# A fused two-block transformer kernel: the second block's first norm taken by halves of the tokens, with its context rows normed ahead

## The reference

```python
# first block, layer 1, its end
x = x + rmsnorm(y, g_post_mix[1]);  h_ = rmsnorm(x, g_pre_ffn[1])
y = conv_ffn(h_, ...)                        # up (2 x 2816 columns), conv, silu*val, down
x = x + rmsnorm(y, g_post_ffn[1])
# second block, layer 0, its start: h = x (512 tokens), hc = ctx (256 tokens)
mx = split(silu(c) @ w_mod[0] + b_mod[0], 6);  mc = split(silu(c_ctx) @ w_mod[0] + b_mod[0], 6)
ax = rmsnorm_2(h,  norm1_g[0]) * (1 + mx[1]) + mx[0]
ac = rmsnorm_2(hc, norm1_g[0]) * (1 + mc[1]) + mc[0]
mixing_layer(ax @ w_in[0], ac @ w_in[0], ...)
```

## Time and profile before

| | before |
|---|---|
| runs | 2862.49, 2864.14, 2866.07 us (median 2864.14) |
| profiled execution | 2862.76 us, its span 2861.0 us |
| TensorE busy | 2795.2 us, 98% |
| VectorE, ScalarE, GpSimd busy | 62%, 40%, 6% |
| HBM traffic | 94 GB/s over the span |

### The profile page before, as it was taken

How to read it: one execution, slowest core, us unless ns; L and a number is a source line. 1 busy time by engine, 2 the same in 40 slices (tenths; PEclk the granted TensorE clock), 3 DMA queues, 4 the chain that set the end, 5 groups by cost and what they waited for, 6 DMA issues and landing times. The chain is left out here.

```text
span 2861.0 us, 35838 instructions
## 1 busy us (share of the span) xinstructions
PE 2795.2 (98%) x14584; PEld 2371.3 (83%) x14584; DVE 1772.3 (62%) x2696; ACT 1141.6 (40%) x1734; POOL 157.8 (6%) x172
## 2 busy tenths in 40 slices
PE   9999999999899999999989999999999999999998
PEld 8658888888477888889956899999998975788887
DVE  6678866678768667676676565335534137674563
ACT  5255524443545334342265333223323236553342
POOL 0101000010210000100020100000000002100001
PEclk9999999999999999999999999999999999999999
DMA  5303242343122342425610121121121121232322
GB/s 208 112 16 125 90 146 97 95 135 124 38 81 90 105 137 94 140 100 206 219 49 30 59 74 64 57 72 59 62 61 64 66 100 52 75 106 84 113 85 85
DMA packets 85205, 269.96 MB, mean 94 GB/s; under 512 B 9264, under 2 KB 14256, under 8 KB 84656
## 3 DMA queue, kind: packets, MB, share of 16 engines
q1 hardware_dynamic: 85040, 267.66, 28.1%
HBM read 265.52 MB, written 2.10 MB: 94 GB/s over the span
## 5 line engine op out<-in xcount | busy, mean ns | idle before, releaser
L1213 PE MATMUL PS<-HH,WH 128*128 128x512 f32 (+2 forms) x3124 | 1027.5, 362 | 16.2 <-DVE HL L849 6.1
L1213 PE MATMUL PS<-HL,WH 128*128 128x512 f32 (+2 forms) x3124 | 1017.3, 359 | 0.0
L1213 PE MATMUL PS<-HH,WL 128*128 128x512 f32 (+2 forms) x3124 | 1017.2, 359 | 0.0
L1009 DVE TENSOR_TENSOR WL<-STAGE,WH 128x1024 fp32r<-128x1024 f32 (+2 forms) x420 | 482.9, 1152 | 465.0 <-ACT WH L1003 464.6
L1003 ACT ACTIVATE WH<-STAGE 128x1024 fp32r<-128x1024 f32 (+2 forms) x420 | 407.9, 974 | 619.2 <-DMA STAGE<-in_w_down 272.7
L1213 PEld LDWEIGHTS PS<-HH,WH 128*128 128x128 f32 x3124 | 577.7, 188 | 91.5 <-DVE HL L849 8.7
L1213 PEld LDWEIGHTS PS<-HL,WH 128*128 128x128 f32 x3124 | 578.6, 188 | 64.5 <-issue 2.4
L1213 PEld LDWEIGHTS PS<-HH,WL 128*128 128x128 f32 x3124 | 578.3, 188 | 63.0
L1213 PE MATMUL PS<-GH,WH 128*128 128x512 f32 (+2 forms) x902 | 301.7, 364 | 0.0
L1213 PE MATMUL PS<-GL,WH 128*128 128x512 f32 (+2 forms) x902 | 300.4, 362 | 0.0
L1213 PE MATMUL PS<-GH,WL 128*128 128x512 f32 (+2 forms) x902 | 300.4, 362 | 0.0
(11 more groups left out here) (233 smaller groups left out, 2434.2 us busy)
## 6 DMA issues: line engine op xcount, KB each, us to landing
STAGE<-in_w_up SPq DMA_DIRECT2D x176, 512.0 KB, 3.2
MODBUF<-in_w_mod SPq DMA_DIRECT2D x96, 512.0 KB, 4.1
STAGE<-in_w_in SPq DMA_DIRECT2D x84, 512.0 KB, 3.3
STAGE<-in_w_down SPq DMA_DIRECT2D x64, 384.0 KB, 3.1
STAGE<-in_w_down SPq DMA_DIRECT2D x64, 320.0 KB, 2.9
STAGE<-in_w_out SPq DMA_DIRECT2D x32, 512.0 KB, 4.4
BM<-in_na_bias SPq DMA_DIRECT2D x24, 256.0 KB, 2.5
CR<-in_const_ret SPq DMA_DIRECT2D x2, 1152.0 KB, 5.2
```

What stands on the lines that cost most here:

```text
L1009: dve.tensor_tensor(WL[unit.slot][:, 0:size], STAGE[unit.slot][:, 0:size], WH[unit.slot][:, 0:size].bitcast(F32), ALU.subtract).then_inc(w ...
L1213: ins = pe.matmul(self.acc(tile, col, tn, p), w[:, c:c + P], r[:, k, t0:t0 + tn], start=(k == 0 and m == 0 and not (joined and p)), stop=( ...
```

## The change

What it does, in five parts:

1. `CrossHead` takes the place of `NormHead` for `norm_in2(0)`, and the last down projection of layer 1 is halved too (`halved=half`). A new `CtxPrep` runs inside that projection: ScalarE squares the context chunks, two in each of tiles 0 to 3; GpSimd adds them, two behind its own add of each of the tiles 1 to 4; TensorE takes their mean at the start of tile 5, waiting for the last of these adds (`csq_added`); and at tiles 4, 5 and 6 the context chunks are normed (T, HH, HL, 256 columns). After the last down tile `CrossHead.begin` first multiplies the context columns for the first three `in2(0)` tiles, with the sums of the squares of X's first half among them, then does half 0 of the tokens with the sums of half 1 between its chunks, then half 1. The idle matmuls of this crossing are gone.
2. `mods`: two products for tiles 1 to 4 of `out1` in place of one for tiles 0 to 5, and two for all 8 tiles of the first down projection of each layer in place of 6. The products of the last down projection of layer 1 are thereby gone from it.
3. The copy to COND and the load of the context move from that last down projection to `out1(1)`; products from then on read COND.
4. Where the token count changes, the accumulators keep their turns, and a tile waits only for the tiles that used its banks.
5. `pe_chunk` takes a part of the columns and whether it is the last; the first three tiles of `in2(0)` have their columns in one piece (`flat`).

```diff
+        class CrossHead(Head):
+
+
+            begins = True
+
+            def __init__(self, scale, shift, hi, lo, gain):
+                super().__init__(hi, lo, SEQ)
+                self.scale, self.shift, self.gain = scale, shift, gain
+
+            def plan(self, run):
+                self.h0, self.t0, self.y0, self.x0, self.before = run.n_h, run.n_t, run.n_y, run.n_x, run.squares
+                self.halved, self.steps, self.joined = True, [], False
+                run.n_h, run.n_t, run.n_y, run.n_x = run.n_h + 24, run.n_t + 24, run.n_y + 16, run.n_x + 16
+                self.ctx_norm = Rstd(run, CTX, [(0, SEQ, CTX)])
+                self.first = Rstd(run, SEQ, self.before.parts)
+                self.norm = Rstd(run, SEQ, self.before.parts)
+
+            def step(self, i):
+
+                return i % DC, slice(SEQ, TOK) if i < DC else self.rows(i // DC - 1), 1 if i < DC else 0
+
...
+            def act(self, act):
+                last = self.before.seg.tiles[-1]
+
+                def squared(i):
+                    p, c = divmod(i, DC)
...
+                        for u in self.early:
+                            self.run.split_high(act, u)
+                        self.before.wait_mean(act, 1)
+                        self.first.act(act, 1)
+                for c in range(2):
+                    squared(DC + c)
+                act.wait_ge(xsq_summed.sem, xsq_summed.at(self.x0 + DC))
+                self.norm.act(act)
+                for c in range(DC):
+                    self.high(act, DC + c)
+                    if c + 2 < DC:
+                        squared(DC + c + 2)
+                act.wait_ge(xsq_summed.sem, xsq_summed.at(self.x0 + 2 * DC))
+                self.norm.act(act, 1)
+                for c in range(DC):
+                    self.high(act, 2 * DC + c)
+
+            def dve(self, dve):
+                last = self.before.seg.tiles[-1]
+
+                def scaled(i):
```

`CrossHead.act` ends as it begins, with `self.high` for half 1. `CrossHead.dve` has the same order in scales, adds, T and HL. Its TensorE part and `CtxPrep`:

```diff
+                              start=(c == 0), stop=(c == DC - 1)).then_inc(xsq_summed.sem, 1)
+
+                ctx(0, first[0:2])
+                ctx(1, first[0:2])
+                self.before.mean(pe, 1)
+                for k in range(2, DC):
+                    if k < 6:
+                        squares_summed(2 * k - 4)
+                        squares_summed(2 * k - 3)
+                    ctx(k, first[0:2])
+                for k in range(DC):
+                    ctx(k, first[2:])
+                for p in range(2):
                     for c in range(DC):
-                        pe.wait_ge(xsq_done.sem, xsq_done.at(self.x0 + c + 1))
-                        for t0, tn in ranges(self.tokens):
-                            ins = pe.matmul(PS[2][:, t0:t0 + tn], MEAN[:], SQ[c % 2][:, t0:t0 + tn],
-                                            start=(c == 0), stop=(c == DC - 1))
-                        ins.then_inc(xsq_summed.sem, 1)
-                    idle(pe, 24, 3)
+                        self.wait_lo(pe, DC + DC * p + c)
+                        for tile in first:
+                            self.run.pe_chunk(pe, tile, c, 0, halves_of(SEQ)[p], final=p == 1)
+                        if p == 0:
+                            squares_summed(DC + c)
...
+            def pool(self, pool, t):
+                if t <= 4:
+                    for c in (2 * t - 2, 2 * t - 1):
+                        if c == 0:
+                            continue
+                        pool.wait_ge(csq_done.sem, csq_done.at(c + 1))
+                        if c > 1:
+                            pool.wait_ge(csq_added.sem, csq_added.at(c - 1))
+                        first = SQ[0] if c == 1 else SQSUM
+                        pool.tensor_tensor(SQSUM[:, SEQ:TOK], first[:, SEQ:TOK], SQ[c % 2][:, SEQ:TOK],
+                                           ALU.add).then_inc(csq_added.sem, 1)
+
+            def pe(self, pe, run, tile):
+                if tile.t == 5:
+                    pe.wait_ge(csq_added.sem, csq_added.at(DC - 1))
+                    pe.matmul(PS[2][:, 0:CTX], MEAN[:], SQSUM[:, SEQ:TOK], start=True, stop=True).then_inc(csq_summed.sem, 1)
 
```

The banks, the products and the copy:

```diff
                         if tiles and tiles[-1].seg.tokens != seg.tokens:
-                            turns, changed, users = 0, len(tiles), {}
+                            behind = 1 + next(i for i, acc in enumerate(columns(TOK)) if tiles[-1].banks[-1] in acc[2])
+                            turns = behind * len(accs) // 3
...
-                            tile.after = max([changed] + [users.get(bank, 0) for bank in banks])
...
+                            tile.after = max(users.get(bank, 0) for bank in tile.banks)
...
+                if keeps:
+                    self.from_x = next(product.n for tile in tiles for product in tile.products if product.kept)
+                    self.mod_loads[tiles[2].units[0].u + ring] = [None]
...
+                            if self.keeps and tile.n == 1:
                                 act.activation(COND[:], X[:, :, SEQ:TOK], ACT.Copy).then_inc(cond_kept.sem, 1)
...
-                            mods=lambda t: 1 if t < 6 else 0, halved=1)]
...
+                            mods=lambda t: 2 if 1 <= t < 5 else 0, halved=1)]
...
-                            ready=half * HALF, mods=lambda t: 2 if t < 6 else 0, out_dve=add_y if half else to_y, squares=y_rows if half else None,
-                            halved=1 if half and l == 0 else 0)]
+                            ready=half * HALF, mods=lambda t, half=half: 2 if half == 0 or t < 6 else 0,
+                            out_dve=add_y if half else to_y, squares=y_rows if half else None,
+                            prep=prep if half else None, halved=half)]
```

More of the change, by code:

```diff
@@ L245, in columns @@
             if tokens == SEQ:
[L246 to L247 removed]
+                return [(PS[i], h * SEQ, [2 * i + h]) for i in (0, 1, 3) for h in range(2)]
+            return [(PS[i], 0, [2 * i, 2 * i + 1]) for i in (0, 1, 3)]
         def tap(seg, t, k):
@@ L800, in act @@
             def act(self, act):
-                n = self.tokens
                 self.before.wait_mean(act)
-                if self.gain:
-                    self.first.act(act)
-                    act.wait_ge(ctx_in.sem, ctx_in.at(16))
-                    for c in range(DC):
-                        act.wait_ge(added.sem, added.at(self.y0 + c + 1))
-                        if c > 1:
-                            act.wait_ge(xsq_summed.sem, xsq_summed.at(self.x0 + c - 1))
-                        act.activation(SQ[c % 2][:, 0:n], X[:, c, 0:n], ACT.Square).then_inc(xsq_done.sem, 1)
-                    act.wait_ge(xsq_summed.sem, xsq_summed.at(self.x0 + DC))
                 self.norm.act(act)
@@ L821, in dve @@
             def dve(self, dve):
-                if self.gain:
-                    self.first.wait(dve)
-                    scale_y(dve, self.gain, 0)
-                    for c in range(DC):
-                        if c + 1 < DC:
-                            scale_y(dve, self.gain, c + 1)
-                        dve.wait_ge(y_scaled.sem, y_scaled.at(self.y0 + c + 1))
-                        dve.tensor_tensor(X[:, c, 0:SEQ], X[:, c, 0:SEQ], Y[:, c, :], ALU.add).then_inc(added.sem, 1)
                 def normed(i):
@@ L914, in __init__ @@
                 self.n_h = self.n_t = self.n_y = self.n_x = self.n_hid = self.n_late = 0
-                self.squares, self.units, tiles, turns, changed, users = None, [], [], 0, 0, {}
+                self.squares, self.units, tiles, turns, users = None, [], [], 0, {}
                 for head, segments in parts:
@@ L949, in __init__ @@
                                 if waiting and waiting[0].l == (seg.weights is a["w_in2"]):
+                                    waiting[0].kept = keeps and tile.n > 1
                                     tile.products.append(waiting.pop(0))
@@ L1198, in dve_out, with pe_chunk @@
                     seg.out_dve(dve, t, tile.ps[:, tile.col:]).then_inc(acc_free.sem, 1)
-            def pe_chunk(self, pe, tile, k, p=None):
+            def pe_chunk(self, pe, tile, k, p=None, part=None, final=True):
                 seg = tile.seg
-                parts = [halves_of(seg.tokens)[p]] if p is not None else parts_of(seg.tokens)
-                joined = tile.t < seg.together and seg.head.steps[-1][0] is None
+                parts = [part or halves_of(seg.tokens)[p]] if p is not None else parts_of(seg.tokens)
+                joined = tile.t < seg.together and seg.head.joined
                 if k == 0 and tile.after:
@@ L1321, in scalar @@
                                 seg.prep.act(act, self, tile)
-                            if any(product.n + 1 == 2 * MOD_N for product in tile.products):
+                            if self.keeps and tile.n == 1:
                                 act.activation(COND[:], X[:, :, SEQ:TOK], ACT.Copy).then_inc(cond_kept.sem, 1)
@@ L2595, in build @@
         stream(run)
```

(5 more changed lines are left out.)

171 lines of the change are left out of this document (138 added, 33 removed).

## The result

| | before | after |
|---|---|---|
| median of 4 runs | 2864.48 us (2862.49 to 2866.07) | 2881.58 us (2880.66 to 2882.23) |
| span of the profiled execution | 2861.0 us | 2880.5 us |

A forecast was written before the change was run, and what follows sets the result against it. TensorE, busy 98% of the span, was taken to bound the kernel. Terms of −0.3 + 6.3 + 4.1 + 4.7 − 0.9 = +13.9, +19 with clock, took 2862.8 to 2881.8, stated as 2883 for the median; range 2868 to 2896.

The forecast's parts named there:

- The wait at tile 5: Last down projection: TensorE waits 5.9 us for context adds queued behind GpSimd's add of tile 4; with the mean, +6.3.
- The pairs: Both out1: two products per tile make VectorE and GpSimd's last add late; +4.1 in out1(0), +4.7 in out1(1) with allowances.
- The crossing: Last down tile to fourth in2(0) tile: idle time becomes a ScalarE/VectorE-bound loop, rounds of 3.2 us; −0.3 net.
- the rival of a low clock there: Crossing: clock stays low through the half-idle rounds, 12 us more, about 2895 to 2900; chance 0.15.
- the rule: From the Trainium skill: GpSimd shares SBUF interfaces with VectorE and contends with its instructions that read two SBUF inputs.
- The allowance for MODBUF: Crossing: the first MODBUF of in2(0), whose transfer takes 4.1 us, could give 0.3 us back.
- The banks: in2(1), at the change of width: the wait of 0.90 us for the evictions goes, −0.9.
- Pairs free: Rival in out1: paired products cost nothing, only 0.15 us remains in each, giving 2873; chance 0.10.
- own pace at the crossing: Rival: squares and HH overlap more, TensorE sets the crossing's pace, up to 14 us go, about 2870; chance 0.08.
- adds in time: Rival at tile 5 and both out1: GpSimd's adds end before TensorE's three waits; 2865, no change; chance 0.05.
- The clock: Lower TensorE clock behind waits: 1.6 us at tile 5, 1.0 behind each out1 wait, 1.5 at the crossing; +5.
- copy and load: out1(1): allowances of 0.3 us each for the copy to COND and the context's load, raising +4.1 to +4.7.

The follow-up runs named there:

- The pairs alone: The kernel before, with only out1 changed to two products for tiles 1 to 4 instead of one for tiles 0 to 5: 2875.91 us.
- the short adds: The changed kernel with GpSimd's adds of the tiles' squares, all but each norm's first, cut to 16 columns: 2873.78 us, 1.0034 of before.

## Why the prediction was right

It said 2883 (2868 to 2896), slower; the measured median is 2881.6. The mechanism was right in its main steps, the closeness of the sum was in part luck. By its own steps:

- **The wait at tile 5.** 5.9 forecast, 5.70 measured, and undoing the order took it away. The nearest row for GpSimd's adds, 0.73, fitted: six of them took 4.4 us.
- **The pairs.** A cycle of 5.12 was forecast and 5.12 measured; the last add was forecast 4.1 later in `out1(0)`, and the wait was 4.2 longer. The pairs alone and the short adds show both halves of the argument, the moved products and the meeting with GpSimd.
- **The crossing.** Rounds of 3.2, then a wait of 2.7, were forecast; 3.25 and 2.59 measured. The whole came to 58.7 us, 1.8 over before, where −0.3 and 1.5 of clock were forecast; the clock cost 1.5. The clock held through the loop, so the rival of a low clock there is out, and fell only behind the 2.59. The context's T and HL did meet GpSimd's adds (an HL of 1.21 us at 1226.98 in place of 0.48, two T of 1.91 at 1233.71 in place of 0.88), as the rule would have it, but TensorE waited for none of them. The allowance for MODBUF wasn't needed.
- **The banks.** −0.9 forecast, and the wait of 0.90 is gone; the stretch around it is 1.2 shorter.
- **The rivals.** Pairs free, own pace at the crossing, adds in time, all fell with these rows.

Two terms were mis-sized. The clock was put at 5 us: 1.0 behind each `out1` wait, 1.6 at tile 5 and 1.5 at the crossing. In `out1` it cost 2.5 each, at tile 5 2.2: a wait of 5 us brought a longer stretch at half clock than the one of 2.71 from which I priced it, and the 1.0 was less even than the 1.6 of that shorter wait. With 1.5 at the crossing that makes 8.7. The excess of 3.6 over the terms' 5.1 was made good by something that the prediction didn't have: at two places of the second block the clock didn't fall any more, 1.5 and 1.6 us less. That was luck, and the sum came out as close as it did by it. And `out1(1)` needs a second reading: 0.6 was added for copy and load, which cost next to nothing beside the pairs and 4.0 without them.

## What to carry to other kernels

A step that is moved to fill an idle engine is to be placed by the queues that it joins: the context's adds had 4.5 us of idle GpSimd ahead of them and were put behind the one add that TensorE's next step didn't need. Where one engine alternates between two halves of a pipeline, write out the circle of waits: here one swap of two ScalarE instructions was worth 9 us at its place. When two causes of a delay hide one another, undo both before counting either.

## What the runs showed of the hardware

- The granted clock's drop behind a gap depends on more than the gap's length. Behind waits of 2.4 to 2.7 us it fell in some profiles and not in others: behind 2.44 us in `out1(1)` with single products (0.63 and 0.52 in the windows of 2 us from 850 and 852), behind 2.59 at the crossing of the kernel after, not behind 2.59 with HH ahead of the square. Behind every wait of 4.5 us or more it fell, in all eight profiles that had one. So the time of a part that no edit touched differed by up to 3 us between profiles; whether the edit or the execution did it isn't shown.
- A loop of 1.48 us standing in rounds of 3.25 us left the clock at 1.00.
- A VectorE instruction with two SBUF inputs that began beside a GpSimd add took longer by a little less than what was left of the add: 0.85 us more with 0.98 left, 0.50 more with 0.63, 0.73 more with 0.93 (the HL at 1226.98, beside an add from 1226.63 for 1.28). A COPY from PSUM at 239.15 in the kernel before, beside an add from 238.83 for 1.55, kept its 0.68.
